# Two transformer blocks in one kernel: weight panels prepared earlier, the first mixer's attention one head behind, and score products over 64 partitions

## What is computed

```python
# first block: ffn, mixer, ffn, each in a sandwich of norms
ffn1 = lambda h: swiglu(h, ffn1_w_gu[l], ffn1_w_down[l])      # "gated": two up products per hidden unit
mix  = lambda h: mixer(h, w_in[l], rel_bias[l], conv_w[l], ...)  # attention of 8 heads of 64, and a gated recurrence
# second block, two layers: a token mixer and a squared-relu MLP
def _diff_attention(dq, dk, dv, lam):
    s = jnp.einsum('bqhjd,bkhjd->bhjqk', dq, dk) * ATTN_SCALE   # two maps j per head, d = 64
    p = jax.nn.softmax(s, axis=-1)
    return jnp.einsum('bhqk,bkhe->bqhe', p[:, :, 0] - lam * p[:, :, 1], dv)
def _gqa_attention(gq, gk, gv):
    s = jnp.einsum('bqhgd,bkhd->bhgqk', gq, gk) * ATTN_SCALE    # two key heads, d = 64
    return jnp.einsum('bhgqk,bkhd->bqhgd', jax.nn.softmax(s, axis=-1), gv)
```

## Time and profile before

| | before |
|---|---|
| median of 3 runs | 4459.82 us (4450.64 to 4469.57) |
| the profiled execution | 4472.22 us, span 4470.3 us |
| PE busy | 3978.6 us (89%), 18628 instructions |
| PEld busy | 3190.3 us (71%) |
| DVE busy | 2296.9 us (51%) |
| ACT busy | 1369.7 us (31%) |
| POOL busy | 1350.3 us (30%) |
| mean granted TensorE clock | 0.943 |

### The profile page before, as it was taken

The page is one execution under the profiler, slowest core; times in us unless marked ns, Lnnn a source line. Parts: engine busy times, 40 slices in busy tenths (PEclk is TensorE's granted clock), DMA queues, the critical chain, the costliest instruction groups (busy, mean ns, idle before and its releaser), DMA issues.

```text
span 4470.3 us, 50814 instructions
## 1 busy us (share of the span) xinstructions
PE 3978.6 (89%) x18628; PEld 3190.3 (71%) x18628; DVE 2296.9 (51%) x3495; ACT 1369.7 (31%) x1832; POOL 1350.3 (30%) x1012
## 2 busy tenths in 40 slices
PE   7999787999997888889879979999887979788999
PEld 6888674877776846757758868888674847667887
DVE  4676735126665263452582257777536252834334
ACT  3222533242224242143122242111324243224223
POOL 1444330433443202102232322332220303444443
PEclk8999898999998999999989989999998989999999
DMA  4454210223332101101111123333110201122222
GB/s 175 166 191 160 74 68 29 103 76 132 141 141 85 54 1 39 51 1 38 57 66 48 61 81 113 113 115 120 47 54 0 80 10 66 68 83 76 97 100 85
DMA packets 57219, 364.66 MB, mean 82 GB/s; under 512 B 5744, under 2 KB 12144, under 8 KB 13936
## 3 DMA queue, kind: packets, MB, share of 16 engines
q1 hardware_dynamic: 42064, 271.11, 17.2%
q10 hardware_dynamic: 15008, 91.49, 5.4%
HBM read 360.49 MB, written 2.10 MB: 81 GB/s over the span
## 4 chain that ended last, share of the span: by engine, by line
issue 66%; POOL 23%; PE 10%; DVE 0%; ACT 0%; POOLq 0%; DVEq 0%; ACTq 0%
POOL b_wlo L558 23%; PE ps L1640 3%; PE ps L1641 3%; PE ps L1642 3%; POOLq L572 0%; ACT ps L613 0%; DVE b_y L1151 0%; DVE b_x L1155 0%; PE ps L1692 0%; DVE b_y L1178 0%; PE ps L1703 0%; ACT b_whi L599 0%; POOLq L574 0%; DVE b_y L1204 0%; PE ps L1716 0%
## 5 line engine op out<-in xcount | busy, mean ns | idle before, releaser
L558 POOL TENSOR_TENSOR b_wlo<-b_raw,b_whi 128x512 fp32r<-128x512 f32 x1008 | 1350.1, 1370 | 3099.6 <-ACT b_whi L599 3099.6
L1640 PE MATMUL ps<-b_hhi,b_whi 128*128 128x512 f32 (+1 forms) x3160 | 1185.4, 375 | 110.2 <-POOL b_wlo L558 45.0
L1641 PE MATMUL ps<-b_hlo,b_whi 128*128 128x512 f32 (+1 forms) x3160 | 1169.0, 370 | 0.0
L1642 PE MATMUL ps<-b_hhi,b_wlo 128*128 128x512 f32 (+1 forms) x3160 | 1167.3, 369 | 0.0
L1640 PEld LDWEIGHTS ps<-b_hhi,b_whi 128*128 128x128 f32 x3160 | 607.1, 192 | 220.6 <-issue 65.5
L599 ACT ACTIVATE b_whi<-b_raw 128x2048 fp32r<-128x2048 f32 x252 | 480.7, 1907 | 743.4 <-PE ps L1642 731.4
L1641 PEld LDWEIGHTS ps<-b_hlo,b_whi 128*128 128x128 f32 x3160 | 607.3, 192 | 98.8 <-issue 1.9
L1642 PEld LDWEIGHTS ps<-b_hhi,b_wlo 128*128 128x128 f32 x3160 | 605.4, 192 | 100.3
L1099 DVE SCALAR_TENSOR_TENSOR b_macc<-b_mraw,b_csil,b_macc 128x256 f32<-128x256 f32 x868 | 508.9, 642 | 7.0
L1204 DVE TENSOR_TENSOR b_y<-ps,b_y 128x512 f32<-128x512 f32 x496 | 335.5, 689 | 263.1 <-PE ps L1642 263.0
L1640 PE MATMUL ps<-b_whi,b_dhi 128*128 128x512 f32 x992 | 397.9, 401 | 41.5 <-DVE b_y L1204 23.6
(11 more groups left out here) (277 smaller groups left out, 4770.8 us busy)
## 6 DMA issues: line engine op xcount, KB each, us to landing
b_raw<-panels SPq DMA_DIRECT2D x252, 1024.0 KB, 4.8
b_mraw<-mod_panels ACTq DMA_DIRECT2D x78, 1024.0 KB, 6.6
b_y<-mod_panels ACTq DMA_DIRECT2D x3, 1024.0 KB, 15.9
b_xin<-xT SPq DMA_DIRECT2D x1, 2048.0 KB, 25.5
b_mraw<-mod_panels SPq DMA_DIRECT2D x2, 1024.0 KB, 18.9
b_rope<-rope ACTq DMA_DIRECT2D x4, 512.0 KB, 3.8
outT<-b_xout SPq DMA_DIRECT2D x4, 512.0 KB, 3.8
b_mod<-mod_panels ACTq DMA_DIRECT2D x1, 1024.0 KB, 20.9
```

The costliest lines, as they stand in the source:

```text
L558: ins = pool.tensor_tensor(wlo[:, s, c], raw[:, s, c], whi[:, s, c].bitcast(F32), ALU.subtract)
L1640: pe.matmul(out, a[0], b[0], start=first, stop=False)
L1641: pe.matmul(out, a[0], b[1], start=False, stop=False)
L1642: return pe.matmul(out, a[1], b[0], start=False, stop=last)
```

## The change

Four things change.

1. `first_ups`, in ffn1 and ffn2 only: the eight k are walked with the first panel alone, which needs only this panel; then the second panel's up products follow as a block of their own.
2. In the recurrent blocks ACT's `split(p + 3)` stands right behind the two Gelus, ahead of the sigmoids. The `split(p + 1)` at the start of the next block then has nothing left to do, since a panel is split once.
3. In the first mixer's attention the scores and transposed tiles of a head are packed into three banks (0 to 2 for even heads, 3 to 5 for odd ones), with the tiles of width 384 and 128 together in one bank; banks 6 and 7 take the weighed output. b_pt has two copies. `weigh` and `keep` run one head later. The order of the row blocks within a head changes with the banks.
4. In the second and third mixer both operands of the score products are cut to the 64 partitions of their own head.

```diff
-            pt = sb("pt", [4, L], F32, s2)
+            pt = sb("pt", [2, 4, L], F32, s2)
...
+    SCORE_ORDER, TURN_ORDER = (2, 0, 1, 3), (1, 3, 0, 2)
+    head_bank = lambda u, w: (3 * (u % 2) + (1, 2, 1, 0)[w - 1], 3 * P if w == 1 else 0)
...
                     act.activation(gy[:, n, :], ps[:, 2 + n, :], ACT.Gelu_apprx_tanh).then_inc(*up("gelu", (r, n)))
+                split(p + 3)
...
             def keep_transposed(u):
-                for j in range(4):
+                for j in TURN_ORDER:
                     act.wait_ge(*at("tr", (u, j)))
-                    if u >= 1:
-                        act.wait_ge(*at("pv", u - 1))
-                    act.activation(pt[:, j, j * P:L], ps[:, 4 * (u % 2) + j, j * P:L], ACT.Copy).then_inc(*up("pt", (u, j)))
+                    if u >= 2:
+                        act.wait_ge(*at("pv", u - 2))
+                    b, c = head_bank(u, 4 - j)
+                    act.activation(pt[:, u % 2, j, j * P:L], ps[:, b, c:c + L - j * P], ACT.Copy).then_inc(*up("pt", (u, j)))
...
-                keep(u)
+                if u >= 1:
+                    keep(u - 1)
                 if u + 2 < HEADS:
                     biased_max(u + 2)
                     normalise(u + 2)
+            keep(HEADS - 1)
...
-                pe.wait_ge(lo_ready, m.p0 + m.UP)
+                pe.wait_ge(lo_ready, m.p0 + 1)
                 for k in range(KD):
                     pe.wait_ge(*at("h_lo", (pre, k)))
-                    for n in range(2):
+                    for n in range(1 if m.gated else 2):
...
+                if m.gated:
+                    pe.wait_ge(lo_ready, m.p0 + 2)
+                    for h in range(2):
+                        for k in range(KD):
+                            ins = up_product(m.p0, 1, h, k)
+                    ins.then_inc(panel_used, 1)
...
             for u in range(HEADS):
                 turn(u)
-                weigh(u)
+                if u >= 1:
+                    weigh(u - 1)
                 if u + 2 < HEADS:
                     scores(u + 2)
+            weigh(HEADS - 1)
...
-                q = qm2[:, j, (i % 4) * P:(i % 4 + 1) * P]
+                o = slice(64 * j, 64 * j + 64)
+                q = qm2[o, j, (i % 4) * P:(i % 4 + 1) * P]
                 if k0 == 0:
-                    pe.matmul(ps[:, b, :], q, keys(u)[:, 0:L], start=True, stop=True)
-                    ins = pe.matmul(ps[:, b + 1, 0:LC], q, keys(u)[:, L:TT], start=True, stop=True)
+                    pe.matmul(ps[:, b, :], q, keys(u)[o, 0:L], start=True, stop=True)
+                    ins = pe.matmul(ps[:, b + 1, 0:LC], q, keys(u)[o, L:TT], start=True, stop=True)
                 else:
-                    ins = pe.matmul(ps[:, b, 0:LC], q, keys(u)[:, L:TT], start=True, stop=True)
+                    ins = pe.matmul(ps[:, b, 0:LC], q, keys(u)[o, L:TT], start=True, stop=True)
```

More of the change, by code:

```diff
@@ L1321, in biased_max @@
                     if u >= 2:
-                        dve.wait_ge(*at("tr", (u - 2, 3)))
+                        dve.wait_ge(*at("tr", (u - 2, TURN_ORDER[-1])))
                     near = max(0, i - 1) * P
                     end = (i + 1) * P
-                    b = 4 * (u % 2) + i
-                    ins = dve.scalar_tensor_tensor(pr[:, u % 2, i, near:end], ps[:, b, near:end], SCALE,
+                    b, c = head_bank(u, i + 1)
+                    ins = dve.scalar_tensor_tensor(pr[:, u % 2, i, near:end], ps[:, b, c + near:c + end], SCALE,
                                                    bias[:, u % 2, 2 * P - (end - near):2 * P], ALU.mult, ALU.add)
@@ L1329, in biased_max @@
                         chain(ins)
-                        ins = dve.tensor_scalar(pr[:, u % 2, i, 0:near], ps[:, b, 0:near], SCALE, pcol("rb_far", u),
+                        ins = dve.tensor_scalar(pr[:, u % 2, i, 0:near], ps[:, b, c:c + near], SCALE, pcol("rb_far", u),
                                                 ALU.mult, ALU.add)
@@ L1348, in keep @@
                 dve.wait_ge(*at("pv", u))
-                src = ps[o:o + 64, 4 * (u % 2), :].rearrange("p (a n) -> p a n", a=2)
+                src = ps[o:o + 64, 6 + u % 2, :].rearrange("p (a n) -> p a n", a=2)
                 hi, lo = hhi[o:o + 64, 2 * t:2 * t + 2, L:TT], hlo[o:o + 64, 2 * t:2 * t + 2, L:TT]
@@ L1910, in scores @@
                 pe.wait_ge(*at("k", u // 2))
[L1911 to L1915, removed]
+                for i in SCORE_ORDER:
+                    b, c = head_bank(u, i + 1)
+                    if i:
+                        claim([b], ("biased", (u, i)))
+                    ins = pe.matmul(ps[:, b, c:c + (i + 1) * P], qm[:, u % 2, i * P:(i + 1) * P], kf[:, u // 2, 0:(i + 1) * P],
+                                    start=True, stop=True)
+                    if i != 2:
+                        ins.then_inc(*up("scores", (u, i)))
+                C.name("scores", (u, 2), *C.labels[("scores", (u, 0))])
             def turn(u):
                 pe.wait_ge(*at("probs", (u, 3)))
-                for j in range(4):
-                    b = 4 * (u % 2) + j
-                    claim([b], ("pt", (u, j)))
+                for j in TURN_ORDER:
+                    b, c = head_bank(u, 4 - j)
+                    if j != 3:
+                        claim([b], ("pt", (u, 3 if j == 1 else j)))
                     for i in range(j, 4):
-                        ins = pe.transpose(ps[:, b, i * P:(i + 1) * P], pr[:, u % 2, i, j * P:(j + 1) * P], const("ident"))
-                    ins.then_inc(*up("tr", (u, j)))
+                        ins = pe.transpose(ps[:, b, c + (i - j) * P:c + (i - j + 1) * P], pr[:, u % 2, i, j * P:(j + 1) * P], const("ident"))
+                    if j != 1:
+                        ins.then_inc(*up("tr", (u, j)))
+                C.name("tr", (u, 1), *C.labels[("tr", (u, 3))])
             def weigh(u):
-                b, t = 4 * (u % 2), u // 2
+                b, t = 6 + u % 2, u // 2
                 claim([b], ("att", u))
@@ L1932, in weigh @@
                     v = x[:, 4 + j // 2, (j % 2) * 512 + t * P:(j % 2) * 512 + (t + 1) * P]
-                    ins = pe.matmul(ps[:, b, j * P:L], v, pt[:, j, j * P:L], start=(j == 0), stop=(j == 3))
+                    ins = pe.matmul(ps[:, b, j * P:L], v, pt[:, u % 2, j, j * P:L], start=(j == 0), stop=(j == 3))
                 ins.then_inc(*up("pv", u))
```

## The result

| | before | with the change |
|---|---|---|
| median | 4459.8 us (4449.9 to 4469.6) | 4471.9 us (4465.0 to 4480.2) |
| the profiled execution, span | 4470.3 us | 4466.5 us |
| mean granted TensorE clock | 0.943 | 0.937 |

The ratio is 1.0027, 95% interval 1.0019 to 1.0034: within 0.5% of no change, and rather slower than faster. The forecast was 4402, range 4382 to 4442. The profiled execution of the change is one of its shorter ones, that of the kernel before (4472.2 us) is longer than all that its median is of; the medians decide. Every ratio in this text is to executions of the kernel before that were taken beside the kernel in question (medians of 4459.8 to 4466.8 us), so it doesn't always follow from 4459.8.

What follows compares the result with a forecast made beforehand. TensorE was taken as the engine to shorten, stopped by waits or, in later attention, full with its own work. 15 + 33 + 20 - 10 = 58 us off the 4459.8 median gave 4402 us, range 4382 to 4442.

Steps and rivals of the forecast that it cites:

- part 4: Second and third mixer's attention: score products over 64 partitions lose 10 us through changes of shape.
- upper bound: Score products: if nothing may be in flight across a change of shape, 200 x 0.24 = 48 us lost.
- the bounds of -17 and 48: Score products over 64 partitions: from 17 us gained by overlap in d to 48 us lost by changes of shape.
- rival (a): Second and third mixer's attention: every change of shape empties TensorE, 48 us lost in place of 10, 4440; chance 0.14.
- the 0.24: Most us per change of shape: 0.16 tail of the product before, 0.08 slower start of an empty engine.
- rival (c): Attention stages: half the rows idle, granted clock falls; over half of these stretches some 200 us lost, 4600; chance 0.06.
- The gain of overlap: Attention in d: two heads' products at once could hide at most 17 us; none was counted.
- Part 2: Recurrent blocks of the first mixer: the early split removes TensorE's waits for POOL's low part, 33 us gained.
- Part 3: First mixer's attention: weighing one head behind, 8.7 us per head for 11.9, 20 us gained, 14 at low clock.
- Part 1: First up products of ffn1 and ffn2: waits of 8 us shrink to 2.0, 15 us gained in all.

Runs made afterwards that it cites:

- burst_64: The change without its 64-partition score products, plus 24 dense 512-column filler matmuls over 64 partitions ahead of g's first scores in both mixers: 4467.3 us, ratio 1.0010.
- parts123: The change with its score products back over 128 partitions, the other three changes kept: 4406.7 us, ratio 0.9870 to before.
- warm_change: The full change plus full-height 512-column filler products (4 in d, 6 in g) ahead of each attention stretch's first scores: 4457.6 us, ratio 0.9985.
- warm_parts123: The change with 128-partition score products, plus full-height filler products (4 in d, 6 in g) ahead of each attention stretch's first scores: 4400.9 us, ratio 0.9861.

## Why the prediction was wrong

**The step that failed is part 4: "I take a fifth of the upper bound: 10 us lost".** It lost 65 (70 by the ratios). Two things were wrong in it.

The change of shape was priced from "the nearest row is scores behind transposes, another change of kind: no gap today". Scores and transposes both use all 128 rows, so no shape changes between them, and that row was no evidence. The price is 0.10 to 0.14 us, and some 25 us in all: between the bounds of -17 and 48, in the direction of rival (a), which was half right. By the Trainium skill, "TensorEngine Tiling (Array Packing)", section Key Properties, a change of the tiling mode drains the engine; the trace agrees in kind, at 0.10 us a change over the kernel, less than half of the 0.24 that I had built from rows for a full drain.

The clock was rival (c), and its mechanism was the right one, at some 40 us instead of 200. I dismissed it (chance 0.06) because "the low-clock pieces seen so far follow idle stretches of PE, and it will be as busy as before". Every busy stretch in that trace ran at full height, so it could not tell busy from high. Its size was too large, since the low clock came for a third of the time (168 of 549 us) and d hides part of it. As a rival it was put at one size, "some 200 us"; a mechanism that was not excluded should have had its small size priced too, and a range up to 4475 would then have held the result. Its threshold was off too: the sum was 58 us of gain, so the sign turns at 58 us of loss, not at 90. The Trainium skill, "TensorE: Matmul & The Clock Gate", Part 1, says that activity releases the clock and gives 2.4 GHz for a busy TensorE. burst_64, 100% busy at 0.50 for 40 us, shows that being busy is not enough, and the measurement decides.

Also, (a) and (c) were treated as alternatives, with one chance each. Both came at once, from the same edit, and only together they cancel the other parts.

**The gain of overlap, taken as none: near, though no kernel tests it by itself.** Two heads' products do run side by side where nothing waits between them; the trace of the change has 11 such starts, less than 0.12 us behind the one before, all in d and most at 1.2 GHz, worth some 5 us as an estimate (11 x 0.4). PE's timeline in d, with the change (the 256-column product of one head and the 512-column one of the other, 0.08 us apart):

```profile
1514.21 0.63 PE L2037 MATMUL ps<-b_dk,b_qm 64*128 64x256 f32 x1
1514.29 1.19 PE L2036 MATMUL ps<-b_dk,b_qm 64*128 64x512 f32 x1
```

It hides one instruction of 0.4 us there, at 1.2 GHz. A product over 64 partitions takes the time of a full one where the clock is equal: 41.29 / 48 = 0.86 us an instruction at 1.2 GHz in burst_64, and two of the first scores of the kernel before take 1.83 (1903.39 to 1905.22, with the start of an empty engine). At the full clock the second 512-column instruction of a score product is followed by the next after 0.43 us in the change and in parts123 alike. The Trainium skill, "TensorE: Matmul & The Clock Gate", says the same of 32 rows in its table of goals.

**Part 2, 33 us: right**, 34 alone. **Part 3, 20 us: a little high**, 14 alone, the value that the forecast had for a PE at the low clock in half of the heads: four periods of 9.2 us instead of 8.7, with most of the score blocks at the low clock (3.97 and 4.11 us, against 2.40). **Part 1, 15 us: wrong**, 4. Its chain had DVE's memsets and "DVE 0.7", but not the modulation in DVE's program ahead of the second unit's multiplication. So most of the wait was moved and not removed: PE waits 12.5 us for POOL in the two ffns together, where it waited 17.1 before. The three were forecast at 68 us and brought 58 (4465.0 - 4406.7). That 4406.7 lies near the 4402 forecast for the whole says nothing for the forecast, which had part 4's loss in it.

## What to carry to other kernels

Cutting a matmul's contraction from 128 to 64 rows saved no time for that matmul, and here it cost 65 us, 0.5 us per row of scores: each switch between the heights showed by 0.1 us, and TensorE could be fully busy and yet be held at 1.2 GHz. So zeros in the other half were the cheaper choice here; a kernel whose products of half the height mostly run side by side was not tried. A mechanism whose evidence is "it hasn't happened while the engine was busy" is only excluded if the engine was busy in the new way too. When a wait is to be hidden, read the whole program order of every engine in its chain up to the next time that the chain is walked; here the load for DVE's side work had lain under the old wait, and without that wait the work came too late. The best kernel of this study is parts 1 to 3 without part 4, 4406.7 us, 1.3% faster than before (with the warm-up 4400.9 us, the same within the intervals).

## What the runs showed of the hardware

- A dense burst of products over 64 partitions kept the granted clock at 0.50 for 41 us; the same burst over 128 reached 1.00 within 7 us. From a full clock, g's half-height scores among transposes brought it down to 0.50 within 2 us of their start and held it there for 25 us (warm_change, third mixer); the full-height ones kept 1.00 (warm_parts123). With half-height scores among full-height transposes without a warm-up the clock rose late (in the second mixer's g at 1878, 24 us into it), and it fell to 0.50 again in mid-stretch, as in this window row of the change:

```profile
1968.00:1973.00 5.00, 5.00 (x8) 2.24 (x8) 1.38 (x3) 1.27 (x3) 0.00 (x0) 0.50 0.01 2
```

- A switch of the height between neighbouring matmuls cost 0.10 us, measured over 256 of them at an unchanged clock (33 and 39 us low in the stretches); in rows of g at the full clock it was up to 0.14 us.
